# One granule of four in the output stage gets its low part from an accumulating transfer

## What is computed

```python
for l in range(DEPTH):                      # DEPTH = 2
    h = _rmsnorm(x, norm_g[l])
    z = h @ w_in[l]
    (rq, rk, rv, rg, gq, gk, gv, gg, ga_f, ga_b, pv, pg, mq, mkv, mkr, mg) = jnp.split(z, points, axis=-1)
    y_a = _retention_branch(rq, rk, rv, rg, ...)
    y_b = _gla_branch(gq, gk, gv, gg, ga_f, ga_b, ...)
    y_c = _pool_branch(pv, pg, ...)
    y_d = _mla_branch(mq, mkv, mkr, mg, ...)
    y = jnp.concatenate([y_a, y_b, y_c, y_d], axis=-1)
    x = x + y @ w_out[l]                    # the output stage
```

## Time and profile before

| | us |
|---|---|
| median of 3 runs | 834.78 |
| lowest and highest | 833.9, 835.31 |
| the profiled execution, its own time | 834.93 |
| its span in the trace | 833.1 |
| TensorE busy | 818.1 (98% of the span) |
| VectorE busy | 456.1 (55%) |
| ScalarE busy | 421.5 (51%) |
| GpSimd busy | 49.3 (6%) |
| granted TensorE clock, mean | 0.998 |

### The profile page before, as it was taken

One profiled execution on the slowest core, in us unless ns is written; L12 is line 12 of the kernel. 1 busy time (PEld: TensorE's weight loads), 2 busy tenths in 40 slices (PEclk: granted clock), 3 DMA queues, 4 the chain that ended last, 5 costly groups with the idle time before them and its releaser, 6 DMA issues.

```text
span 833.1 us, 11231 instructions
## 1 busy us (share of the span) xinstructions
PE 818.1 (98%) x3980; PEld 691.2 (83%) x3980; DVE 456.1 (55%) x591; ACT 421.5 (51%) x604; POOL 49.3 (6%) x43
## 2 busy tenths in 40 slices
PE   6999999999999999999989999999999999999998
PEld 4898888888888888888869888888878888888886
DVE  1564487544473953645345635964553659546552
ACT  4855566545725543433357655664576254444341
POOL 5110000000000001000122000000000010010000
PEclk9999999999999999999999999999999999999999
DMA  9765764434534454566536657644344445536664
GB/s 345 264 220 184 239 221 164 160 127 130 199 127 152 154 175 152 193 210 197 159 126 228 240 194 226 202 154 152 126 152 152 152 152 188 172 121 215 191 188 137
DMA packets 41924, 150.80 MB, mean 181 GB/s; under 512 B 4752, under 2 KB 4880, under 8 KB 41744
## 3 DMA queue, kind: packets, MB, share of 16 engines
q1 hardware_dynamic: 40592, 145.25, 52.3%
q0 software_dynamic: 432, 3.02, 0.9%
q10 hardware_dynamic: 848, 1.83, 0.7%
HBM read 147.98 MB, written 2.10 MB: 180 GB/s over the span
## 4 chain that ended last, share of the span: by engine, by line
PE 97%; DMA 1%; issue 1%; ACT 1%; DVE 1%; SPq 0%; DVEq 0%; ACTq 0%
PE pair L361 86%; PE bank L392 4%; PE bank L679 1%; PE bank L504 1%; PE bank L669 1%; PE bank L604 1%; DMA raw<-stream 1%; PE bank L638 0%; PE bank L574 0%; PE bank L633 0%; PE bank L552 0%; PE bank L564 0%; ACT work L910 0%; DVE lo L967 0%; PE bank L475 0%
## 5 line engine op out<-in xcount | busy, mean ns | idle before, releaser
L967 DVE TENSOR_TENSOR lo<-raw,hi 128x1024 fp32r<-128x1024 f32 (+3 forms) x266 | 307.4, 1178 | 222.0 <-ACT hi L713 218.6
L713 ACT ACTIVATE hi<-raw 128x1024 fp32r<-128x1024 f32 (+3 forms) x272 | 270.5, 1022 | 157.2 <-PE pair L361 130.7
L361 PE MATMUL pair<-hi,xT_hi 128*128 128x512 f32 (+1 forms) x768 | 295.5, 395 | 3.4 <-ACT xT_hi L747 2.7
L361 PE MATMUL pair<-lo,xT_hi 128*128 128x512 f32 (+1 forms) x768 | 296.3, 386 | 2.3 <-DVE xT_lo L984 2.3
L361 PE MATMUL pair<-hi,xT_lo 128*128 128x512 f32 (+1 forms) x768 | 296.8, 386 | 0.0
L361 PEld LDWEIGHTS pair<-lo,xT_hi 128*128 128x128 f32 x768 | 145.1, 189 | 30.2 <-issue 3.2
L361 PEld LDWEIGHTS pair<-hi,xT_hi 128*128 128x128 f32 x768 | 144.2, 189 | 30.7 <-ACT xT_hi L747 3.3
L361 PEld LDWEIGHTS pair<-hi,xT_lo 128*128 128x128 f32 x768 | 144.9, 189 | 28.5
L361 PE MATMUL pair<-hi,yT_hi 128*128 128x512 f32 (+1 forms) x304 | 116.7, 384 | 0.0
L361 PE MATMUL pair<-hi,yT_lo 128*128 128x512 f32 (+1 forms) x304 | 116.6, 383 | 0.0
L361 PE MATMUL pair<-lo,yT_hi 128*128 128x512 f32 (+1 forms) x304 | 116.5, 383 | 0.0
(11 more groups left out here) (137 smaller groups left out, 470.4 us busy)
## 6 DMA issues: line engine op xcount, KB each, us to landing
raw<-stream SPq DMA_DIRECT2D x272, 512.0 KB, 4.2
out<-x SPq DMA_DIRECT2D x8, 256.0 KB, 5.0
consts<-consts_in POOLq DMA_DIRECT2D x1, 1922.0 KB, 15.5
mats<-mats_in ACTq DMA_DIRECT2D x2, 576.0 KB, 3.7
x<-x_in POOLq DMA_DIRECT2D x2, 512.0 KB, 9.6
x<-x_in SPq DMA_DIRECT2D x1, 512.0 KB, 4.7
x<-x_in ACTq DMA_DIRECT2D x1, 512.0 KB, 10.0
consts<-consts_in ACTq DMA_DIRECT2D x1, 64.0 KB, 4.4
```

The source lines that it names most:

```text
L361: return nc.tensor.matmul(pair[a][m][:, 0:width], x_part[:, slots[i], m * P:(m + 1) * P], w_part[r][:, i * 512:i * 512 + width], start=(sl ...
L713: nc.scalar.activation(cut[0], cut[1], ACT.Copy).then_inc(rounded[r].sem, 1)
L967: nc.vector.tensor_tensor(cut[0], cut[1], cut[2].bitcast(F32), ALU.subtract).then_inc(split[r].sem, 1)
```

## The change

In the output stage every granule in slot 3 (107, 111, ... 135, eight in a layer) no longer gets its `lo` from VectorE. ScalarE, after it has rounded `hi[3]`, copies `raw[3]` a second time with a scale of -1 into `lo[3]`: the negated high part. GpSimd waits for that and issues a transfer from `raw[3]` to `lo[3]` which adds to what is there (`accum_op=ALU.add`), waits until it has landed, and signals `split[3]` in VectorE's place. VectorE skips these granules. GpSimd's loop over the layers is written out, so that the transfers stand in its program one by one.

```diff
+BY_DMA = [j for j in range(GRANULES) if PLAN[j][0].startswith("out") and j % RING == RING - 1]
...
+        negated, lo_landed = signal("negated", len(BY_DMA)), signal("lo_landed", 16 * len(BY_DMA))
...
                         nc.scalar.activation(cut[0], cut[1], ACT.Copy).then_inc(rounded[r].sem, 1)
+                        if j in BY_DMA:
+                            nc.scalar.activation(lo[r][:], raw[r][:], ACT.Copy, scale=-1.0).then_inc(negated.sem, 1)
...
                     for j in range(pos[0], upto):
+                        if j in BY_DMA:
+                            continue
                         r = j % RING
                         dve.wait_ge(*rounded[r].at(l, j // RING + 1))
...
-            with pool.Fori(0, DEPTH) as l:
+            for l in range(DEPTH):
...
                 rsqrt(o_ms, o_rs, oa_ms_ready, oa_rs_ready)
+                for n, j in enumerate(BY_DMA):
+                    r = j % RING
+                    pool.wait_ge(*negated.at(l, n + 1))
+                    pool.dma_start(lo[r][:].bitcast(F32), raw[r][:], accum_op=ALU.add).then_inc(lo_landed.sem, 16)
+                    pool.wait_ge(*lo_landed.at(l, 16 * (n + 1)))
+                    pool.sem_inc(split[r].sem, 1)
```

## The result

The changed kernel takes 867.33 us (median of 4 runs, 861.53 to 868.55) against 834.82 us: a ratio of 1.0375, 95% interval 1.0351 to 1.0399. It is slower by 32.5 us. The prediction was 880 us, range 841 to 925: right in its direction and in what TensorE would wait for, 12.7 us too high in its size. The profiled execution took 866.77 us, its span 865.0 us.

The account below looks back on a forecast made before the run. The prediction took TensorE's stream to bound the kernel. Stalls of 8D - 33.5 = 22.5 us a layer, 45.0 us in two layers, on 834.9 us gave 880 us, range 841 to 925.

Parts of the forecast that it names:

- The bound: Whole kernel: TensorE's stream bounds it, busy 98% of the span; time that VectorE saves gains 0.
- What was costed at nothing: Output stage: sixteen more ScalarE copies, GpSimd's issuing and written-out loop, next layer's first subtractions, output adds: 0 on the path.
- D: Slot 3 in the output stage: time from the negation's end until the slot counts as split, 7.0 us.
- base: Part of D: a 512 KB transfer from issue to landing, 4.2 us, the median; GpSimd's slower issue adds 0.4.
- second operand: Part of D: the add must read lo as well as raw, 1.6 us more.
- overlap with the loads: Part of D: held-back loads go out in a burst and are still in the engines, an estimated 0.6 us.
- The first two granules: Granules 107 and 111 of a layer: stalls of D - 3.5 and D - 2.4, or 3.5 and 4.6 us.
- The loop: Granules 115 to 135: load, rounding, negation and D last 13.3 us against 10.9; six stalls of 2.4 us a layer.
- the prediction's own sign of an error in the loop's terms: Output stage: the loop's terms are wrong if the landing of raw moves away from 4.2 us.
- The short transfer: Rival: raw lands at 3.2, D 5.2, loop 10.5 us; only first two stalls remain, 844 us; chance 0.23 (839 to 864).
- The slow add: Rival: D is 10 us, the add being slow or sharing engines with loads; 928 us; chance 0.23 (over 904).
- Not slower: Rival: the slack swallows the transfer, D at or below 2.4, a landing of 1.8 us; 835 us; chance 0.04.

Follow-up runs that it names:

- the sparse kernel: The changed kernel with the transfer for granules 115, 123 and 131 alone, three a layer; 843.22 us, ratio 1.01 to the kernel before.
- the smaller load: The changed kernel, but from granule 104 on slot 3's loads bring only 128 of 1024 columns; 854.93 us, ratio 1.0246 to the kernel before.
- the plain copy: The changed kernel with the same transfers copying raw over lo in place of adding to it; 846.94 us, ratio 1.0129 to the kernel before.

## Why the prediction came out as it did

**The bound.** Right. VectorE's 18.5 us are worth nothing, and the kernel with all of the change but the transfer is at 0.9997 of before.

**What was costed at nothing.** Right, by the same run: the second copy on ScalarE, GpSimd as go-between, its written-out loop, the start of the second layer, and the output additions.

**D.** The sum was 7.0 us; in the changed kernel it is 0.3 to the issue, a landing of 5.1 in the median (4.5 to 7.5), and 0.1 to TensorE's start: 5.5. Its terms missed in opposite directions. The *base* of 4.2 us with 0.4 for GpSimd's issue was taken from loads out of HBM beside their own like; a copy inside the core lands after 2.9 us with its issue. That term was 1.7 too high. The *second operand*, 1.6 us, was right: 4.5 against 2.9. The *overlap with the loads*, 0.6 as an estimate, is 2.0 us where the ring runs undisturbed (6.5 in the sparse kernel against 4.5), and 0 to 3 in the loop. Two errors of 1.7 and 1.4 cancel by luck within a running ring, where D is 6.9; in a ring that already stands the transfers are less disturbed and D is smaller. The fit of the Trainium skill (DMA: Bandwidth & Descriptors, anatomy of a SWDGE transfer), which with the bytes doubled gave D near 5.0, describes the lone transfer (4.5 and 0.4) well and misses the one beside the stream by 2 us. Its 843 us need the loads at 3.2 us too; with a landing of 4.2 the steps give 8 x 5.0 - 33.5 = 6.5 us a layer, 848. That both source reads count in full, by the Trainium skill (Collectives: The Full Stack, why ReduceScatter is half of AllGather), agrees with the 2.72 us of the engines here against 1.28, a little more than twice.

**The first two granules.** Predicted 3.5 and 4.6 us a layer, measured 2.1 and 2.7 in the first layer and 2.0 and 2.7 in the second (start to start). The formulas D - 3.5 and D - 2.4 give 2.1 and 2.6 with the D that these two had in the first layer (5.18 and 4.56 of landing, and 0.4): right in form, too high by D. Taking them out gave back 12.6 us, with the falls of the clock that followed them.

**The loop.** Predicted six stalls of 2.4 us a layer, measured 6.3 and 8.2 us for six, some 1.2 each. The step that failed beside D is the landing of raw. The median 4.2 of the earlier trace rows is that of a load which meets the one before it; when a stalled slot is released little is in the engines, and slot 3's load lands after 3.2 to 3.5 us in eleven of fourteen cases (5.0 to 6.4 in the others). In the turn that the chain shows, D is 6.0 and the loop 11.5 us, and not 13.3. The loads of the other slots went the other way, as this view of the second layer shows:

```profile
DMA to landing us min/median/max: 3.2/5.3/7.6
```

With a median of 5.3 the landing of raw has moved away from 4.2, the prediction's own sign of an error in the loop's terms; but the other slots have slack, and TensorE waits for none of them in the stages. That slot 3's load is a link of the loop is shown by the smaller load (stalls of 14.6 us down to 6.8). It is not the only way round: when the load is fast, the same loop closes over TensorE's own twelve matmuls, a third of a microsecond shorter (5.48 us from a split to the next issue against 5.83). And part of these stalls needs no loop at all: in the sparse kernel a transfer by itself costs 0.6 to 1.1 us, its D of 6.9 against 6.1.

**What was missed.** The falls of TensorE's clock, some 6.5 us in the profiled execution, and the slow second matmul behind each stall, 1.5. They stand against an overestimate of the stalls of 45.0 - 24.0 = 21.0 us. So the 12.7 us by which the forecast was too high are the difference of a larger error and an omission, and that it came this near is in part luck.

**The rivals.** The short transfer had the landing of raw right (3.3) and its own D nearly (5.2 against 5.5), but gave 844 us, since it let the loop close below the ring's turn; half a microsecond decides there, and the stretch by the loads is more. The slow add is refuted: 4.5 us alone. Not slower would have needed a landing of 1.8 us; even the plain copy takes 2.9.

## What to carry to other kernels

Before a step in a ring of buffers is given to a transfer, add up the whole loop that the slot goes through (transfer, release, reload, preparation) and hold it against the time that the consumer takes for one turn; hold the transfer by itself against its own slack as well, for in the sparse kernel that alone was short. Take the transfer's latency beside the stream that it will share the engines with: here 2 to 3 us of 6.5 to 7.5 came from the stream, an earlier start did not remove them, and half the bytes did only in part. And relieve an engine only if somebody waits for it.

## What the runs showed that I had not expected

- An accumulating transfer of 512 KB inside the core lands after 4.5 us alone, a copy after 2.9; in time of all engines 2.72 and 1.28 us, a load from HBM 1.58. Half of it (256 KB) lands after 3.3 us alone.
- Beside loads at some 180 GB/s the accumulating one takes 6.1 to 6.6 us, and up to 7.5 in a burst; half of it takes 3.9 to 7.5 us beside them.
- Stalls of TensorE of over 2 us can bring its clock down to the lower level for 3.41 us, at 1.6 us each, but not each of them does: in one execution's stages it fell four times in six such stalls, in another's once, at the same sum of waits (21.8 us). Why it falls at one and not at the other was not settled.
